# Four moves in the instruction order of a two-layer encoder step: the one-hot compare, expert 1's row turns, the pooling columns, the first stick-breaking logits

## The reference, cut to what matters

```python
def token_mixers(xn, pos, p, hist):
    u_pool, c_q, c_kv, k_r, q_sb, k_sb, v_sb, gate_pre = split_cols(xn @ p["w_in"], IN_SPLITS)
    y_pool = pool_mix(u_ext, pos, p["w_pool_lin"], p["pool_scale"])   # trailing means over 2/4/8/16, minus self
    q = rmsnorm(rope part and rest of (rmsnorm(c_q) @ w_uq)); k, v = mla_keys(...)
    y_mla = softmax attention, 8 heads, chunk mask
    y_sb  = stick-breaking attention, 4 heads:
            z = q k / 8;  a = exp(log_sigmoid(z) + reverse cumulated log_sigmoid(-z))
    h = sum of sigmoid(gate) * (branch @ w_br);  return h @ p["w_out"]

def hier_moe(xn, p):
    # best group of 4, best two of its 4 experts, weights combine[...]
    for e in range(N_EXPERTS):          # 16
        h = silu(xn @ w_exp_gate[e]) * (xn @ w_exp_up[e])
        out = out + combine[..., e:e + 1] * (h @ w_exp_down[e])

x = x + token_mixers(rmsnorm(x)); x = x + hier_moe(rmsnorm(x))
```

## Time and profile before

| | |
|---|---|
| median of 3 runs (lowest, highest) | 1607.18 us (1605.19, 1614.24) |
| the profiled execution's own time | 1608.43 us |
| its span, first to last instruction | 1606.7 us |
| busy: PE, DVE, ACT, POOL | 1404.4 (87%), 767.7 (48%), 623.5 (39%), 105.4 (7%) us |
| mean granted TensorE clock | 0.927 of 2.4 GHz |
| DMA | 229.52 MB, mean 143 GB/s |

### The profile page before, as it was taken

How to read it: one execution, slowest core, us unless ns; L and a number is a source line. 1 busy time by engine, 2 the same in 40 slices (tenths; PEclk the granted TensorE clock), 3 DMA queues, 4 the chain that set the end, 5 groups by cost and what they waited for, 6 DMA issues and landing times.

```text
span 1606.7 us, 21198 instructions
## 1 busy us (share of the span) xinstructions
PE 1404.4 (87%) x8518; PEld 1145.6 (71%) x8518; DVE 767.7 (48%) x1121; ACT 623.5 (39%) x966; POOL 105.4 (7%) x128
## 2 busy tenths in 40 slices
PE   5988889899999958989479888899999999499992
PEld 5984556699999846666279745577999987366661
DVE  4326316633334356767353281265333344577763
ACT  5326524522224134545243274244222232355550
POOL 0310010000000000000203001000000000100002
PEclk9999799899999969999889997998999999699996
DMA  7231300032126357997722102000332153599955
GB/s 249 66 122 41 105 0 1 1 106 87 50 84 226 130 199 291 369 350 285 223 113 66 58 18 87 0 1 2 105 104 88 46 221 131 209 344 377 364 201 193
DMA packets 95928, 229.52 MB, mean 143 GB/s; under 512 B 14410, under 2 KB 64612, under 8 KB 82916
## 3 DMA queue, kind: packets, MB, share of 16 engines
q1 hardware_dynamic: 83252, 179.58, 31.8%
q0 software_dynamic: 7360, 29.89, 5.3%
q10 hardware_dynamic: 5232, 18.88, 2.9%
HBM read 197.69 MB, written 34.84 MB: 145 GB/s over the span
## 4 chain that ended last, share of the span: by engine, by line
PE 73%; DVE 10%; ACT 8%; DMA 5%; issue 2%; POOL 1%; ACTq 1%; POOLq 0%; SPq 0%; DVEq 0%
PE ps L757 9%; PE ps L759 9%; PE ps L758 9%; PE ps L1178 6%; PE ps L919 4%; DVE ew_r L1626 3%; DMA rows_back<-xrow_d,row_of 3%; PE ps L1006 3%; PE ps L1069 2%; PE ps L1071 2%; PE ps L1070 2%; PE ps L783 2%; PE ps L785 2%; PE ps L784 2%; PE ps L1145 2%
## 5 line engine op out<-in xcount | busy, mean ns | idle before, releaser
L1626 DVE TENSOR_TENSOR work<-work,ps 128x544 f32<-128x544 f32 x48 | 34.6, 721 | 213.4 <-ACT work L1481 213.4
L1481 ACT ACTIVATE work<-ps 128x544 f32<-128x544 f32 x48 | 30.0, 625 | 249.5 <-PE ps L759 249.5
L758 PE MATMUL ps<-xn_r,ksv_r 128*128 128x272 f32 x384 | 113.1, 295 | 0.0
L758 PE MATMUL ps<-xn_r,work_r 128*128 128x272 f32 x384 | 110.8, 288 | 0.0
L1158 PE MATMUL ps<-ew_r,rows_tok_r 128*128 128x512 f32 x256 | 103.2, 403 | 0.0
L707 POOL DMA_INDIRECT rows_back<-xrow_d,row_of x32 | 34.0, 1063 | 1009.7 <-DVE row_of L1955 768.3
L784 PE MATMUL ps<-wr_r,qt_ht_r 128*128 128x256 f32 (+1 forms) x320 | 93.4, 292 | 0.0
L783 PE MATMUL ps<-work_r,qt_ht_r 128*128 128x256 f32 x240 | 72.9, 304 | 14.0 <-DVE rows_lo_r L1626 7.9
L1626 DVE TENSOR_TENSOR ew_r<-ew,gu_hi_a_r 128x2048 fp32r<-128x2048 f32 x32 | 73.1, 2291 | 16.8 <-ACT gu_hi_a_r L1502 16.8
L758 PEld LDWEIGHTS ps<-xn_r,ksv_r 128*128 128x128 f32 x384 | 74.8, 195 | 0.0
L758 PEld LDWEIGHTS ps<-xn_r,work_r 128*128 128x128 f32 x384 | 72.2, 188 | 0.0
(11 more groups left out here) (342 smaller groups left out, 4041.5 us busy)
## 6 DMA issues: line engine op xcount, KB each, us to landing
wr<-in_w_in SPq DMA_DIRECT2D x68, 512.0 KB, 4.8
ew<-in_w_exp_gate SPq DMA_DIRECT2D x32, 1024.0 KB, 6.5
ew<-in_w_exp_up SPq DMA_DIRECT2D x32, 1024.0 KB, 9.8
ew<-in_w_exp_down SPq DMA_DIRECT2D x32, 1024.0 KB, 8.9
wr<-in_w_out SPq DMA_DIRECT2D x16, 512.0 KB, 4.2
rows_d<-yo_a ACTq DMA_DIRECT2D x16, 512.0 KB, 7.9
rows_d<-yo_b ACTq DMA_DIRECT2D x16, 512.0 KB, 7.6
xres_d<-x_keep SPq DMA_DIRECT2D x2, 2048.0 KB, 7.7
```

Source lines behind the costliest of these rows:

```text
L758: mm(out_[h], w_hi, x_lo[:, c], start=False, stop=False, skip_group_check=True)
L1626: return v_.tensor_tensor(o_, a, b, op)
```

## The change

Four moves; no instruction is added or dropped.

1. The DMAs and the columns of chunks 4 and 5 change places: the pooling columns are chunk 4, the queries chunk 5. TensorE turns `hist` ahead of both chunks, and waits for VectorE's copy of it (`h_ev`) ahead of chunk 5, which now uses bank 7. ScalarE copies `u` out first, from banks 0 to 3, and `qs` after it.
2. `z_products(0)` moves ahead of the last tile's turns (n = 11), and ScalarE's `softplus_tail(0)` ahead of the last `kq_evac(11)`. The wait for `kq_ev` 12 now stands ahead of `z_products(1)`.
3. `turn_rows(1)` moves into the middle of `gate_up(0)`, between its slices 3 and 4; ScalarE's `rows_high(1)` moves ahead of `gate(0)`, and VectorE's `row_number(2)` behind `rows_low(1)`.
4. VectorE's `one_hot(e+3)` moves from the end of iteration e to right behind `act_out(e-1)`.

```diff
-                cols(4, "w_in", C_QS, 256)
-                cols(5, "w_in", C_POOL, 256)
+                cols(4, "w_in", C_POOL, 256)
+                cols(5, "w_in", C_QS, 256)
...
                 pe.wait_ge(tk_ev[0], at(tk_ev, l, 20))
+                pe.wait_ge(smalls[0], at(smalls, l, 288))
+                pe.wait_ge(gpre[0], at(gpre, l, 2))
+                stand(pe)
+                for m in range(2):
+                    ins = nc.tensor.transpose(bank(7, 16, P, 16 * m), hist[0:16, P * m:P * m + P], ident[0:16, 0:16])
+                ins.then_inc(h_tr[0], 1)
                 for c in (4, 5):
...
+                    if c == 5:
+                        pe.wait_ge(h_ev[0], at(h_ev, l, 1))
...
                     m = KM[n] if n < 7 else TM[n - 7]
+                    if n == 11:
+                        pe.wait_ge(kq_raw[0], at(kq_raw, l, 12))
+                        z_products(0)
                     pe.wait_ge(kq_n[0], at(kq_n, l, n + 1))
...
-                pe.wait_ge(kq_ev[0], at(kq_ev, l, 12))
-                pe.wait_ge(kq_raw[0], at(kq_raw, l, 12))
...
-                z_products(0)
+                pe.wait_ge(kq_ev[0], at(kq_ev, l, 12))
                 z_products(1)
...
                     for k in range(DC):
+                        if between and k == DC // 2:
+                            between()
...
-                    gate_up(e, e % 2, e % WS)
+                    gate_up(e, e % 2, e % WS, between=(lambda: turn_rows(1, 1)) if e == 0 else None)
...
-                    if e + 1 < NE:
+                    if e and e + 1 < NE:
                         turn_rows(e + 1, (e + 1) % 2)
...
-                kq_evac(11)
...
+                act.wait_ge(kq_ss[0], at(kq_ss, l, 12))
                 softplus_tail(0)
+                kq_evac(11)
                 softplus_tail(1)
...
                 rows_high(0, 0)
+                rows_high(1, 1)
                 for e in range(NE):
                     gate(e, e % 2)
-                    if e + 1 < NE:
+                    if e and e + 1 < NE:
                         rows_high(e + 1, (e + 1) % 2)
...
-                    if e + 2 < NE:
-                        row_number(e + 2, *((2 + (e - 1) % 2, 508) if e else (7, 4)))
+                    if e and e + 2 < NE:
+                        row_number(e + 2, 2 + (e - 1) % 2, 508)
                     if e:
                         act_out(e - 1, (e - 1) % 2)
+                    if e + 3 < NE:
+                        one_hot(e + 3)
...
                         rows_low(e + 1, (e + 1) % 2)
+                    if e == 0:
+                        row_number(2, 7, 4)
...
-                    if e + 3 < NE:
-                        one_hot(e + 3)
```

More of the change, by code:

```diff
@@ L812, in _ @@
                 pe.wait_ge(qs_ev[0], at(qs_ev, l, 2))
-                pe.wait_ge(smalls[0], at(smalls, l, 288))
-                pe.wait_ge(gpre[0], at(gpre, l, 2))
-                stand(pe)
-                for m in range(2):
-                    ins = nc.tensor.transpose(bank(7, 16, P, 16 * m), hist[0:16, P * m:P * m + P], ident[0:16, 0:16])
-                ins.then_inc(h_tr[0], 1)
                 g = 0
@@ L879, in kq_products @@
                     ins.then_inc(kq_mm[0], 1)
-                kq_products(0)
-                kq_products(1)
-                for n in range(12):
-                    if n < 10:
-                        kq_products(n + 2)
-                    m = KM[n] if n < 7 else TM[n - 7]
-                    pe.wait_ge(kq_n[0], at(kq_n, l, n + 1))
-                    if n >= 2:
-                        pe.wait_ge(kq_ev[0], at(kq_ev, l, n - 1))
-                    if m < P:
-                        stand(pe)
-                    for h in range(HEADS):
-                        ins = nc.tensor.transpose(bank(4 + 2 * (n % 2) + h // 4, m, QK, P * (h % 4)),
-                                                  kw[0:m, n % 3, QK * h:QK * h + QK], ident[0:m, 0:m])
-                    ins.then_inc(kq_tp[0], 1)
-                pe.wait_ge(kq_ev[0], at(kq_ev, l, 12))
-                pe.wait_ge(kq_raw[0], at(kq_raw, l, 12))
                 zf = ps[:, :, :].rearrange("p b n -> p (b n)")
@@ L916, in z_products @@
                     ins.then_inc(z_mm[0], 1)
+                kq_products(0)
+                kq_products(1)
+                for n in range(12):
+                    if n < 10:
+                        kq_products(n + 2)
+                    m = KM[n] if n < 7 else TM[n - 7]
+                    if n == 11:
+                        pe.wait_ge(kq_raw[0], at(kq_raw, l, 12))
+                        z_products(0)
+                    pe.wait_ge(kq_n[0], at(kq_n, l, n + 1))
+                    if n >= 2:
+                        pe.wait_ge(kq_ev[0], at(kq_ev, l, n - 1))
+                    if m < P:
+                        stand(pe)
+                    for h in range(HEADS):
+                        ins = nc.tensor.transpose(bank(4 + 2 * (n % 2) + h // 4, m, QK, P * (h % 4)),
+                                                  kw[0:m, n % 3, QK * h:QK * h + QK], ident[0:m, 0:m])
+                    ins.then_inc(kq_tp[0], 1)
                 def add(h, w, lo, src, n):
@@ L1146, in turn_rows, with gate_up @@
                     ins.then_inc(xg_tr[0], 1)
-                def gate_up(n, s, i):
+                def gate_up(n, s, i, between=None):
                     pe.wait_ge(gu_dn[0], at(gu_dn, l, n * 2 + 2))
@@ L1321, in _ @@
                     act.wait_ge(cm_mm[0], at(cm_mm, l, m + 1))
-                    f(halves(qs[:, m, :]), banks(2 * m), ACT.Copy, scale=0.125).then_inc(qs_ev[0], 1)
-                for m in range(2):
-                    act.wait_ge(cm_mm[0], at(cm_mm, l, m + 3))
-                    b = (4, 6)[m]
+                    b = (0, 2)[m]
                     f(u[:, m, UP:UP + HALF], ps[:, b, 0:HALF], ACT.Copy).then_inc(u_ev[0], 1)
@@ L1328, in _ @@
                     f(u[:, m, US:US + DEC], ps[:, b + 1, SEQ - HALF:HALF], ACT.Copy).then_inc(u_ev[0], 1)
+                for m in range(2):
+                    act.wait_ge(cm_mm[0], at(cm_mm, l, m + 3))
+                    f(halves(qs[:, m, :]), banks(4 + 2 * m), ACT.Copy, scale=0.125).then_inc(qs_ev[0], 1)
                 act.wait_ge(smalls[0], at(smalls, l, 288))
```

## The result

Five runs of each on one chip: 1594.50 us median after (1588.03 to 1596.45) against 1609.42 us before (1605.19 to 1614.24), ratio 0.9903 with a 95% interval of 0.9883 to 0.9923. That is 14.9 us faster; 31.2 were forecast, and 1594.5 lies 3.5 us above the range. The profiled execution took 1596.45 us, its span 1594.7 us.

The account below looks back on a forecast made before the run. TensorE, holding 73% of the last-ending chain, was taken as the bound, through its idle and lower-clock time. 12.5 + 4.5 + 0.5 + 13.7 = 31.2 us off 1608.43, with the median 1.25 lower, gave 1576.0 us; range 1563 to 1591.

Parts of the forecast that it names:

- Move 1: Pooling branch: pooling columns first remove TensorE's idle 4.65 and 4.24 us and keep the full clock; 12.5 us, both layers.
- Move 2: Start of stick-breaking: first logits before the last tile's turns let suffix(0) start earlier, 2.3 us a layer, 4.5 in all.
- the same seven matmuls at 1.00 take 3.0 us: Start of stick-breaking: the moved first logits, z_products(0), take 3.0 us at full clock, 4.4 if the clock falls.
- Move 3: Experts: expert 1's turns inside expert 0 remove 2.46 us idle, but TensorE waits 2.9 us for gather 2; 0.5 us.
- Move 4: Experts: the earlier compare removes 24 waits, 21.2 us, shortening the period from 11.23 to 10.35 us; 13.7 us net.
- the term for late gathers: Experts: gathers landing beyond the shorter period's 9.5 us take 7.5 us off the 21.2 us of compare waits gained.
- (a): Experts: the DMA queues bound them, periods stay near 11.2 us, the compare's move gives nothing; 1589.7 us, chance 0.15.
- (b): Whole kernel: everything yields, no gather is late and the clock stays up; 49.7 us gained, 1557.5 us, chance 0.10.
- (c): Experts: the compare costs each gather 2 us while GpSimd prepares it, so the kernel is slower; 1632 us, chance 0.04.
- (d): Pooling and first logits: those moves don't do what they say, TensorE is held and the clock falls; 1593 us, chance 0.05.
- Waits on `rows_back` of 5 to 12 us in all: Experts: sign that would show the forecast right, TensorE's waits for gathered rows totalling 5 to 12 us.
- Two more signs: Experts: forecast wrong if GpSimd's issue exceeds 0.94 us with the compare, or the lower clock returns more than twice a layer.

Follow-up runs that it names:

- run 6: Run 5's kernel with move 1 undone (query columns first, old rows turned behind both chunks): 1584.33 us, ratio 0.9838 to the kernel before.
- run 8: Also spelled eg_no3: run 5's kernel with move 3 undone (expert 1's rows turned behind expert 0): 1573.01 us, ratio 0.9776 to the kernel before.
- run 3: Changed kernel, from expert 4 on without loading half the gate and up weights and three quarters of the down columns: 1567.28 us, ratio 0.9751.
- run 5: Also spelled early_gather: changed kernel with row numbers multiplied, and gathers issued, one expert product earlier from expert 3 on: 1572.69 us, ratio 0.978.
- run 10: eg_z1 with expert 2's row numbers multiplied inside gate_up(0), ahead of expert 1's turns, its compare and copy moved up: 1557.44 us, ratio 0.9695.
- eg_z1: Run 5's kernel with the second head's logits right behind the first's, ahead of the last tile's turns: 1568.29 us, ratio 0.9747.
- eg_no2: Run 5's kernel with move 2 undone (first logits behind all twelve tiles again): 1573.63 us, ratio 0.9787 to the kernel before.

## Why the prediction was wrong, step by step

- **Move 1, 12.5 us.** Right. No idle time, full clock, and 11.6 us by run 6 (9 by the ratios). The traces agree: the key products of layer 0 start at 120.8 to 122.3 us in every kernel with the move and at 127.1 to 128.4 in every one without it.
- **Move 2, 4.5 us.** Mechanism half right, value wrong: 0.9 us, which can't be told from nothing. In layer 0, on the old scale, `suffix(0)` was forecast at 181.4 or 182.7 and came at 184.8. The step that failed: "the same seven matmuls at 1.00 take 3.0 us", or 4.4 "if the clock falls on the way". The clock fell at once, behind the 2.19 us of idle time ahead of the last full turns, and they took 5.7 us. In layer 1 the clock held and `suffix(0)` did come 2.2 us earlier. What isn't in the sum at all is the give-back further on: between `suffix(0)` and the scores TensorE needed 2.5 us more than before in layer 0 and 3.0 in layer 1. From the first key product to the scores that makes 113.8 and 111.6 us, against 110.8 in both layers before.
- **Move 3, 0.5 us.** Right in size as far as can be told (0.3 by run 8) and in mechanism: a wait of 2.48 us in layer 0 and 2.57 in layer 1 for gather 2 in the changed kernel, 2.9 forecast.
- **Move 4, 13.7 us.** This is the miss: 3.0 us (under 5 by the ratios too). The 21.2 us of compare waits were counted rightly (21.1 gone), and so was the unhindered period (10.35 forecast, 10.18 measured). The step that failed is the term for late gathers, the 7.5 us taken off the 21.2: it was mis-sized. Without the waits for gather 2 (5.05 us) those for gathers 3 to 13 come to 22.2 - 5.05 = 17.1 us, against 1.4 before: 15.7 more. Nine of these 22 gathers were late, by 1.9 us each, which is 0.78 us on average over all of them, where the forecast had 0.18 to 0.38. Of the 5.4 us that this leaves, 3.0 reached the end; behind the longer waits the clock fell. Two things were off. The margin was 9.16 us, not 9.5. Above all, landings were taken from a kernel in which few gathers met the weights of a shorter period, spread "evenly" from 7.2 to 10.6, plus 0.5. They went up to 12.1 with medians of 10.1 and 9.3, and the late ones took 9.9 to 12.1. An average over an even spread hides that. What lengthened them is the weights' traffic (run 3); why the last packets of a gather are held up so much longer than the others is not shown.
- **The sum.** 11.6 + 0.9 + 0.3 + 3.0 = 15.8 us by the runs, 14.9 measured, 31.2 forecast; 10.7 of the difference are move 4, 3.6 move 2. The agreement of 15.8 with 14.9 is partly luck: moves 1 to 3 were measured on another kernel, and each term has an error of several us.
- **Rivals.** (a) would have given 1589.7, near the result, for a wrong reason: the queues moved 401 GB/s, and in run 5 they kept a period of 10.20. (b), with everything yielding, 1557.5, is the time that run 10 reached, but by three further edits (early gathers, second logits, gather 2), so the agreement is luck. (c) didn't occur. Of (d) the part on move 2 did, the clock falling anyway; the part on move 1 didn't.
- **The signs named.** "Waits on `rows_back` of 5 to 12 us in all" could not have held as it stands, since the kernel before had 16.9 us already, 15.6 of them for gather 0. Leaving gather 0 out, they were 22. Two more signs went against the forecast as it had said: GpSimd's issue rose over 0.94 us (1.07), harmlessly, and the lower clock came back in layer 1's experts three times.

## What to carry to other kernels

When a period gets shorter, every transfer that is issued and awaited within one period loses that much margin: compare the new margin with the slowest landings beside full traffic, and don't average over a spread of landings. A wait can make the next transfer early and so hide half of itself; look for an alternation of periods before reading a mean. What such a transfer needs is an earlier issue, not a shorter one: some 5 us of lead on the row numbers were worth 20 to 22 us here. And a step moved up is worth nothing where the next thing it needs stays where it was (gather 2, the second logits).

## What the runs showed of the hardware

- A gather of 128 rows of 4 KB landed in 4.1 to 5.2 us with little other traffic (gather 1 and the last two of a layer), in 5 to 6.3 beside 1.25 MB an expert, in 6.8 to 12.1 beside 3 MB an expert.
- GpSimd's issue of such a gather took 0.94 us alone, 1.07 where VectorE's 0.82 us compare was still running, 2.20 beside a 2.29 us subtraction of two SBUF operands, 2.94 to 3.00 where that subtraction had just begun. In all runs, with one gather for an exception, the issue beside a compare or a subtraction took what was left of VectorE's instruction and 0.81 to 0.89 us: 1.39 + 0.81 = 2.20 (the subtraction of 646.69 to 648.97, the issue at 647.58), and 0.25 + 0.81 = 1.06 beside the compare of 727.80 to 728.62 (the issue at 728.37). The Trainium skill, "SBUF — State Buffer", section "SBUF: two separate sides", has a VectorE instruction with two SBUF inputs and a GpSimd instruction that reads SBUF (as the gather reads its row numbers) exclude each other from a shared port for the whole of the one that started first; these rows agree with that.
- Three kernels in which TensorE waits for gathers 0 and 2 alone repeat closely: 0.9 us between the fastest and slowest run of early_gather and of eg_no3, 1.5 of eg_z1, against 9 us for before. But not all do: eg_no2 has 10 us. What makes the clock differ between runs of one kernel is open.
